# Attention's input as two streams of weight tiles, and VectorE in place of GpSimd in scan preparation

## The reference

```
h    = rms_norm(x) * (1 + scale) + shift          # 768 tokens, width 1024
z    = h @ w_in                                   # 384 for cq, 256 for ckv, 64 for kr
kv   = (rms_norm(ckv) * g_kv) @ w_ukv             # 8 heads: kn (128), v (128)
q    = (rms_norm(cq) * g_q) @ w_uq                # 8 heads: qn (128), qr (64); latent tokens only
qr   = x*cos + swap(x)*sin; kr likewise on the latent tokens
s    = (qn . kn + qr . kr) * 192**-0.5;  o = softmax(s) @ v;  y = o @ w_out
x    = x + gate * y
```

## Time and profile before

| | us |
|---|---|
| three runs | 3564.31, 3566.92, 3569.33 |
| median | 3566.92 |
| the profiled execution | 3562.46 |
| its span, first to last instruction | 3560.7 |
| TensorE matmul busy, share of the span | 2831.6, 80% |
| VectorE | 1563.3, 44% |
| ScalarE | 1012.2, 28% |
| GpSimd | 902.3, 25% |

### The profile page before, as it was taken

How to read it: one execution, slowest core, us unless ns; L and a number is a source line. 1 busy time by engine, 2 the same in 40 slices (tenths; PEclk the granted TensorE clock), 3 DMA queues, 4 the chain that set the end, 5 groups by cost and what they waited for, 6 DMA issues and landing times. The chain is left out here.

```text
span 3560.7 us, 61608 instructions
## 1 busy us (share of the span) xinstructions
PE 2831.6 (80%) x24886; PEld 2277.1 (64%) x24886; DVE 1563.3 (44%) x2380; ACT 1012.2 (28%) x1536; POOL 902.3 (25%) x500
## 2 busy tenths in 40 slices
PE   2668668858577558696778789999994779999998
PEld 2655447638467447684677668888883644467886
DVE  7755825663543255564553433413414124335242
ACT  3231212232221222125222344412213222245232
POOL 3320103114121322120312132222322210044444
PEclk9887759969688779897889899999997889999999
DMA  4410014400000205351000211211110100022222
GB/s 160 169 55 1 1 59 173 149 1 3 2 3 3 94 13 189 112 200 50 3 2 3 101 48 59 72 53 64 63 49 18 50 25 0 24 66 96 92 94 89
DMA packets 59962, 223.43 MB, mean 63 GB/s; under 512 B 5488, under 2 KB 11760, under 8 KB 57712
## 3 DMA queue, kind: packets, MB, share of 16 engines
q1 hardware_dynamic: 59760, 220.51, 17.8%
HBM read 210.00 MB, written 10.49 MB: 62 GB/s over the span
## 5 line engine op out<-in xcount | busy, mean ns | idle before, releaser
L2561 POOL TENSOR_TENSOR f_wl<-f_stage,f_wh 128x1024 fp32r<-128x1024 f32 (+1 forms) x120 | 316.2, 2635 | 627.6 <-ACT f_wh L2557 627.6
L2644 PE MATMUL f_ps<-h_h,f_wh 128*128 128x512 f32 (+1 forms) x1056 | 379.2, 360 | 3.5 <-DVE h_l L2752 2.4
L2644 PE MATMUL f_ps<-h_l,f_wh 128*128 128x512 f32 (+1 forms) x1056 | 377.2, 358 | 0.0
L2644 PE MATMUL f_ps<-h_h,f_wl 128*128 128x512 f32 (+1 forms) x1056 | 377.2, 358 | 0.0
L2557 ACT ACTIVATE f_wh<-f_stage 128x1024 fp32r<-128x1024 f32 (+1 forms) x120 | 137.6, 1146 | 599.6 <-PE f_ps L2644 598.5
L2849 DVE SCALAR_TENSOR_TENSOR f_xr<-f_ps,cols,f_xr 128x511 f32<-128x511 f32 (+1 forms) x132 | 83.1, 657 | 340.1 <-ACT f_xr L2842 339.5
L2644 PEld LDWEIGHTS f_ps<-h_h,f_wh 128*128 128x128 f32 x1056 | 199.6, 189 | 40.1 <-DVE f_xr L2854 3.6
L2644 PEld LDWEIGHTS f_ps<-h_l,f_wh 128*128 128x128 f32 x1056 | 199.7, 189 | 32.0
L2644 PEld LDWEIGHTS f_ps<-h_h,f_wl 128*128 128x128 f32 x1056 | 199.7, 189 | 31.9 <-issue 0.2
L2644 PE MATMUL f_ps<-f_f_ah,f_wh 128*128 128x512 f32 (+1 forms) x528 | 183.7, 355 | 0.0
L2644 PE MATMUL f_ps<-f_f_ah,f_wl 128*128 128x512 f32 (+1 forms) x528 | 183.5, 354 | 0.0
(11 more groups left out here) (691 smaller groups left out, 6962.8 us busy)
## 6 DMA issues: line engine op xcount, KB each, us to landing
f_stage<-in_ffn_up SPq DMA_DIRECT2D x88, 512.0 KB, 3.4
f_stage<-in_ffn_down SPq DMA_DIRECT2D x32, 704.0 KB, 4.1
p_hgrn_mm_side_w<-in_ada_w SPq DMA_DIRECT2D x12, 1024.0 KB, 5.0
qkv_mm_side_w<-in_ada_w SPq DMA_DIRECT2D x12, 1024.0 KB, 5.0
u_mm_side_w<-in_ada_w SPq DMA_DIRECT2D x11, 1024.0 KB, 5.0
mod_w<-in_mod_w SPq DMA_DIRECT2D x8, 1024.0 KB, 14.1
a_uv_mm_side_w<-in_ada_w SPq DMA_DIRECT2D x8, 1024.0 KB, 5.0
p_hgrn_mm_stage<-in_w_in SPq DMA_DIRECT2D x12, 512.0 KB, 4.0
```

Of the source, the lines that this page charges most:

```text
L2561: self.nc.gpsimd.tensor_tensor(self.wl[:, slot, :kt * P], self.stage[:, slot, :kt * P], self.wh[:, slot, :kt * P].bitcast(F32), ALU.subtra ...
L2644: done = self.nc.tensor.matmul(out[s][:, :tn], w, x[:, k, t0:t0 + tn], start=k == 0 and n == 0, stop=k == job.kt - 1 and n == 2)
```

## The change

1. `f0` gets an `Rms` too (squares, sums, variance and `root` of its result), as `f1` had. `FULL_BY_DVE` is (1, 4, 6) in place of (1, 4), for every `Feed`.
2. The stage `c_in` (`latent_flow`) replaces `rms_c`, `cq_mm`, `ckv_mm`, the norm of ckv: a `Feed`, then one `Row` of two kv tiles, the `kr` tile and three `cq` tiles (latent tokens). The norm of kv runs between them (`Small`: squares on ScalarE, variance after the `kr` tile on TensorE, logarithm and exponential on ScalarE, gain on VectorE, high part on ScalarE, rest on VectorE). At the end of its weight loads SyncE stores all of `x` to DRAM, and `x`, `hh` and `hl` leave SBUF after the stage.
3. The stage `c_heads` (`heads_flow`) replaces `cq_rms`, `q_mm`, `kn_mm`, `values` and `rope`: one `Row` of 8 `kn` tiles (evacuated by VectorE), 4 double value tiles (each 6 token groups by 256 outputs, 36 products; ScalarE evacuates), 4 `qr` tiles, 2 `qn` tiles, 6 `qn` tiles. The norm of cq has its variance behind the `kn` tiles. One rotation product (`kr`) comes before the `qr` tiles, four (`qr`) between the second and third `qn` tile, each after VectorE has read the one before; VectorE does all three elementwise passes.
4. `out_flow` for `c_out` loads the latent part of `x` back, behind its first two weight tiles; VectorE waits for it ahead of the first residual.
5. In `rwkv_prepare` and `gdn_prepare` GpSimd's four products go to VectorE, in its order of work.

```diff
@@ rwkv_prepare, VectorE (the same two products leave GpSimd)
             dve.wait_ge(exp_ok, 2)
             nc.vector.tensor_tensor(w["at"][:, :, :], w["kk"][:, :, :], sg[:, :, :], ALU.mult)
+            dve.wait_ge(exp_ok, 3)
+            nc.vector.tensor_tensor(w["kh"][:, :, :], km[:, :, :], rest[:, :, :], ALU.mult).then_inc(kh_ok, 1)
+            dve.wait_ge(kh_ok, 1)
+            nc.vector.tensor_tensor(w["bh"][:, :, :], a[:, :, :], rest[:, :, :], ALU.mult)
@@ gdn_prepare, VectorE (the same two leave GpSimd)
+            nc.vector.tensor_tensor(w["attn"][:, :, :, :], w["kkq"][:, :, :, 0, :], spread(spread(incl, 1, GW), 1, TT),
+                                    ALU.mult).then_inc(masked, 1)
             dve.wait_ge(scaled, 1)
...
             nc.vector.tensor_tensor(w["attn"][:, :, :, :], w["attn"][:, :, :, :], dec[:, :, :, :], ALU.mult)
+            nc.vector.tensor_tensor(w["kdt"][:, :, :, :], w["ktok"][:, :, :].rearrange("p i (h k) -> p i h k", h=GW),
+                                    spread(w["kd"][:, :, r0:r0 + GW], 3, HV), ALU.mult)
@@ Row.load
+        if between:
+            lo += 2
+            span_loop(sp, job.g0, lo, one)
+            for dst, src, moved in between:
+                sp.dma_start(dst, src).then_inc(moved, 16)
@@ out_flow
+            if also:
+                dve.wait_ge(moved, 16 * len(also))
             row.on_dve(dve, job)
@@ ffn_flow
-        rms = Rms(nc, t, st, "rms", x, KD, lo, T, 1e-6, root, sq=xr[:, 0:2], acc=full[:, 1]) if out is not None else None
+        rms = Rms(nc, t, st, "rms", x, KD, lo, T, 1e-6, root, sq=xr[:, 0:2], acc=full[:, 1])
@@ latent_flow (new)
+        @block.sync
+        def _(sp):
+            for job in row.jobs:
+                row.load(sp, job)
+            sp.dma_start(x_dram, x[:, :, :]).then_inc(kept, 16)
+            sp.wait_ge(kept, 16)
+        @block.tensor
+        def _(pe):
+            row.credits(pe)
+            open_clock_with(nc, t, row.ps[3], 12)
+            row.products(pe, to_kv, feed.ready)
+            row.products(pe, to_kr)
+            norm.variance(pe)
+            row.products(pe, to_cq)
+        @block.scalar
+        def _(act):
+            feed.on_act(act, range(0, 2))
+            row.high(act, 0, 0, KD * P)
+            feed.on_act(act, range(2, KD))
+            row.high(act, 1, 1, KD * P)
+            row.on_act(act, to_kv)
+            norm.squares(act, row.banks_free, 3)
+            row.on_act(act, to_kr)
+            norm.inverse_root(act)
+            norm.highs(act)
+            row.on_act(act, to_cq)
@@ heads_flow (new)
+        @block.sync
+        def _(sp):
+            row.load(sp, to_kn)
+            sp.dma_start(table[:, :, :], t["dram"]["rope_table"]).then_inc(table_in, 16)
+            sp.dma_start(swap[:, :], t["dram"]["rope_swap"]).then_inc(table_in, 16)
+            for job in row.jobs[1:]:
+                row.load(sp, job)
+        @block.tensor
+        def _(pe):
...
+            open_clock_with(nc, t, row.ps[3], 12)
+            row.products(pe, to_kn)
+            norm.variance(pe)
+            for g in range(to_v.g0, to_v.g0 + to_v.n):
+                one_value(pe, g, g % 2)
+            pe.wait_ge(table_in, 32)
+            turn(0, kr[:, 0, CTX:])
+            row.products(pe, to_qr, norm.ready)
+            row.products(pe, to_qn[0])
+            pe.wait_ge(row.banks_free, to_qr.g0 + to_qr.n + 2)
+            for n, x in enumerate(rope):
+                turn(n + 1, x)
+            row.products(pe, to_qn[1])
+        @block.scalar
+        def _(act):
+            row.open(act, row.high)
+            norm.squares(act, None, 0)
+            row.on_act(act, to_kn)
+            norm.inverse_root(act)
+            norm.highs(act)
+            for job in row.jobs[1:]:
+                row.on_act(act, job)
+        @block.vector
+        def _(dve):
...
+            for n, x in enumerate([kr[:, 0, CTX:], *rope]):
                 dve.wait_ge(swapped, n + 1)
+                if n:
+                    dve.wait_ge(rope_ok, n)
+                nc.vector.tensor_tensor(part[:, :], turned[:, :], table[:, 1, :], ALU.mult).then_inc(sin_ok, 1)
+                nc.vector.tensor_tensor(x, x, table[:, 0, :], ALU.mult).then_inc(cos_ok, 1)
                 dve.wait_ge(sin_ok, n + 1)
                 dve.wait_ge(cos_ok, n + 1)
+                nc.vector.tensor_tensor(x, x, part[:, :], ALU.add).then_inc(rope_ok, 1)
```

More of the change, by code:

```diff
@@ L2538, in __init__, with width_at, load @@
                 job.act_done = st.sem(f"act_done{n}")
-    def kt_at(self, g):
-        return next(job.kt for job in self.jobs if g < job.g0 + job.n)
+    def width_at(self, g):
+        return next(job.width for job in self.jobs if g < job.g0 + job.n)
     def banks_of(self, job, slot):
         return self.ps[2 * slot + 2 - len(job.spans):2 * slot + 2]
-    def load(self, sp, job):
+    def load(self, sp, job, between=()):
         def one(g, slot):
             sp.wait_ge(self.w_low, g + 1)
-            tile = job.w_tiles[bass.ds(g + (job.first - job.g0), 1)].rearrange("a p f -> p (a f)")
-            sp.dma_start(self.stage[:, slot, :job.kt * P], tile).then_inc(self.w_loaded[slot], 16)
-        span_loop(sp, job.g0, job.g0 + job.n, one)
@@ L2899, in _ @@
         def _(sp):
-            row.load(sp, job)
+            row.load(sp, job, [(dst, src, moved) for dst, src in also])
         @block.tensor
@@ L3131, in _ @@
+            feed.on_pool(pool, range(KD))
+            row.low(pool, 1, 1, KD * P)
+            for job in row.jobs:
+                row.on_pool(pool, job)
         @block.vector
         def _(dve):
[L3133 to L3149 removed]
+            feed.on_dve(dve)
@@ L3164, in _ @@
+        @block.scalar
[7 more added lines that the diff above has]
+                row.on_act(act, job)
+        @block.gpsimd
+        def _(pool):
+            row.open(pool, row.low)
+            for job in row.jobs:
+                row.on_pool(pool, job)
         @block.vector
         def _(dve):
-            dve.wait_ge(loaded, 32)
@@ L3409, in second @@
         late = ExitStack()
+        root = keep("root", [P, T], where=late, side="right")
         x2 = keep("x_b", [P, KD, T], where=late, side="right")
@@ L3457, in second @@
-            rotate(nc, t, [qr[:, f, :] for f in range(HEADS // 2)] + [kr[:, CTX:]])
-            attention(nc, t, qn, qr, kn, kr, v, hh[:, :, :LAT], hl[:, :, :LAT])
-        root = root[:, CTX:]
-        out_flow(nc, t, "c_out", d["mla_w_out"], x2, hh, hl, ((0, LAT),), both[1:], mods, 64, root)
+                cq_h, cq_l = (keep(name, [P, 3, LAT], F32R, where=low) for name in ("c_cq_h", "c_cq_l"))
+                heads_flow(nc, t, d, kv_h, kv_l, kr, cq, cq_h, cq_l, qs, kn, v)
+            late = ExitStack()
@@ new lines, in second @@
+            hh = keep("hc_h", [P, KD, T], F32R, where=late, side="right")
+            hl = keep("hc_l", [P, KD, T], F32R, where=late, side="right")
+            attention(nc, t, qn, qr, kn, kr[:, 0, :], v, hh[:, :, :LAT], hl[:, :, :LAT])
+        x2 = keep("x_c", [P, KD, T], where=late, side="right")
+        root = keep("root_c", [P, LAT], where=late, side="right")
+        out_flow(nc, t, "c_out", d["mla_w_out"], x2, hh, hl, ((0, LAT),), both[1:], mods, 64, root,
+                 also=[(x2[:, :, CTX:], x_dram[:, :, CTX:])])
```

304 lines of the change are left out of this document (161 added, 143 removed).

## The result

Over four runs each, the changed kernel took 3468.85 us (median; 3464.35 to 3478.56) and the kernel before 3565.69 (3564.31 to 3569.33). The ratio is 0.9736, with a 95% interval of 0.9721 to 0.9751. The forecast took 3566.92 us for the kernel before; on that the ratio gives 3472.8. That is inside the range of 3470 to 3497, but 1.2 under the 3474 to 3489 of the forecast's own case. The profiled execution took 3469.12 with a span of 3467.3, against 3560.7: 93.4 less.

A forecast was written before the change was run, and what follows sets the result against it. No engine fills the span; stages with barriers bound the kernel. 80.8 us saved by the streams and feeds plus 4.8 by scan preparation, 85.6 in all, taken from the median 3566.92, gave 3481 us, range 3470 to 3497.

The forecast's parts named there:

- the forecast's own case: Whole kernel: terms add as counted, 3481 us, own range 3474 to 3489, chance 0.65.
- The region's sum: From `f0`'s last residual to `att`'s first work: 156.4 us against 236.4, so 80.0 saved.
- My third rival: Slower than before: idle gaps keep the clock at 1.2 GHz through both streams, 3582 us; chance 0.02.
- scan preparation: `rwkv` and `gdn` preparation, GpSimd's products to VectorE: 8.4 saved, 3.6 lost, together 4.8 us saved.
- Better than counted: No clock loss, rotations at TensorE's pace, second `gdn` direction free, a little at barriers: 3470 us; chance 0.13.
- tail of `f0`: From `f0`'s last residual to the next stage's first work, with the norm's end: 6.5 us, as after `ab_out`.
- `c_in` to the end of its second tile: Start of `c_in`, priced from `f0`'s 36.1 us less 0.6 for the feed block on VectorE: 35.5 us.
- its four rotations: In `c_heads`, four rotation products at VectorE's pace: 7.2 us, plus 1.0 for the clock falling behind the gaps.
- the third value tile's split: In `c_heads`, behind ScalarE's norm: ready 7.9 us after the variance, wanted at 8.5, so hidden.
- the queue rival: Both streams: their queues make TensorE wait, 0.9 us per pair of tiles and 5 more, 3497 us; chance 0.18.
- The table loads: Two in `f0`'s tail, 1.28 us each; the Trainium skill's drain, not seen in the trace, would add 2.8 us.
- Feeds: Feed block 6 moved from ScalarE to VectorE: 0.6 us saved in `c_in`, 0.6 in `f0`, 0.2 in `f1`.

The follow-up runs named there:

- `gdn` only: The kernel before with only gdn_prepare changed, its two GpSimd products moved to VectorE: 3569.26 us, ratio 1.0016.
- `rwkv` only: The kernel before with only rwkv_prepare changed, its two GpSimd products moved to VectorE: 3554.70 us, ratio 0.9975.
- the streams alone: The changed kernel with both halves of scan preparation as in the kernel before: 3466.62 us, ratio 0.9725.
- both edits of `c_heads`: The changed kernel with four warming products instead of twelve and the four rotation products spread between `qn` tiles: 3459.38 us, ratio 0.9707.
- the idle stage: The changed kernel with a stage of 12 GpSimd memsets between `c_heads` and `att`, TensorE idle: 3492.33 us, ratio 0.9799.

## Why the prediction was nearly right

**The step that failed is a term that was missing.** The region's sum ends with "Barrier to `att` 0.7"; everything behind was taken as unchanged. Attention gave 8.6 of the 93.4 us, since TensorE now enters it after work and not after waits. My third rival looked at the clock only inside the new streams. The kernel before showed the other half: 0.83 in the region, and the same in attention's first 46 us, a window that the forecast did not look at.

**The total was nearer than its terms.** Between the two profiled executions 85.6 us were forecast and 93.4 measured. The 7.8 between are 8.6 for attention, 2.5 for the region and 1.5 for `f0`, less the 4.8 of scan preparation, which did not show in that trace. So part of the nearness is luck: a missing gain stood against one that was given back. The result lies between the forecast's case and "Better than counted" at 3470, but of that rival's reasons only the clock behind the feed held; the rotations kept VectorE's pace and the second `gdn` direction was not free.

**The region** came out at 153.9 against 156.4, term by term:

| step | counted | measured |
|---|---|---|
| tail of `f0` | 6.5 | 6.65 |
| `c_in` to the end of its second tile | 35.5 | 34.0 |
| rest of `c_in` | 28.7 | 28.4 |
| barrier | 1.25 | 1.3 |
| `c_heads` | 83.7 | 82.7 |
| its four rotations, in this | 7.2 + 1.0 | 7.9 |
| barrier to `att` | 0.7 | 0.8 |

The first tiles of `c_in` were taken from `f0` with its clock loss of the earlier trace rows; they took 34.0 us, as the first two tiles of `f0` now do, without that loss (see Feeds). The opening of `c_heads` took 10.5 and not 12.2: its 24 matmul records ran closer to the full clock, which they found already open. The rotations wait for VectorE as counted (three waits of 0.78 to 1.71 us). One of them is longer because the middle pass took 1.32 us, not 0.7, beside a low part on GpSimd.

**Costed at nothing, and nothing:** the store of `x` (landed in 11.1 us; 24 us of the stage were left at its issue), its reload (10.6 us; the first residual at 18.15), the norms beside the tiles, and the third value tile's split. That split and its low part were ready at 2784.1, 8.1 us after the variance where 7.9 was counted and 8.5 allowed. TensorE has no wait there. That settles the queue rival: in both streams of the changed kernel TensorE's one wait for a low part is of 0.16 us, at the second tile of `c_in` (1.0 in three of the other traces). The rival's own turn of 3.9 us was shorter than the 4.2 of a pair of tiles, so its loss of 0.9 a pair had no row behind it.

**The table loads** cost 1.28 us each and nothing behind: 2676.60 + 1.28 is 2677.88, and the next work waits 0.35 us for TensorE's variance alone; the second load starts right after that work, and the exponential starts at 2680.59, where the second load ends. The drain of about 1.38 us that the Trainium skill names ("ScalarE: Activation LUTs", What ACT_TABLE_LOAD costs) does not show in this tail, which is 6.65 long.

**Feeds:** `f0` gained 2.1 where 0.6 was counted, all of it in its first two tiles. The tile on VectorE is 0.6 to 0.7 of it, as counted. The other 1.5 goes with the clock behind the feed. With the old feed `f0` takes 576.1 us in the kernel before and in `gdn` only, where the clock at the second tile is 0.69, but 574.5 in `rwkv` only and 574.6 with the tile back on ScalarE, where it is 1.00 and 0.99. In all nine traces with the new feed the clock is 1.00 there and `f0` takes 573.9. So the old feed lost the clock in two executions of four, the new one in none of nine.

**Scan preparation:** 8.4 - 3.6 was counted; alone they measure 8.9 and -5.7. In `gdn` the first direction was mis-sized: 1.4 more instead of 0.5, since the differences are done 6.5 us after the first operation and not 5.5. The second, 2.9, was counted as 3.1. The net is 3.2 us by the two medians and 4.8 by the rows of the stages; it can't be seen between the whole change and the streams alone.

## What to carry to other kernels

A stage in which TensorE mostly waits costs twice: its own length, and a lower clock in the stage behind it. So when such a stage goes, look at the windows of the next unchanged one, and count what it would take at full clock (here 8.6 us less; an idle stage put back made it 15.3 more). Moving work from GpSimd to VectorE pays where it unblocks a long VectorE pass (the bonus, 10.91 to 1.28) and costs where VectorE's own sum is the path. Price edits below 10 us by the length of their own stages, and by the stages behind them over several traces; a whole time or a single trace can't.

## What was not expected of the hardware

Five traces (the changed kernel twice, and the three kernels that alter only `c_heads`) run the same instructions up to `f0`, and reach it at 2091.9, 2099.4, 2100.4, 2101.8 and 2105.8 us: 14 us of spread. Most of it arises between the end of the second `rwkv` preparation and the first `gdn` preparation, a stretch of the same code in every kernel here: 713.8 to 724.2 us in these five, up to 726.7 in all thirteen. Which of its stages it lies in was not followed.

Attention's first 46 us ran at 1.00 (the changed kernel), 0.85 (both edits of `c_heads`), 0.83 (the kernel before) and 0.65 (the idle stage), with TensorE busy throughout in each, and attention took 0, 7.7, 8.6 and 15.3 us longer in all. In the next 46 us the granted clock was 1.00 in all four.
